# The queries' squares summed in two rounded passes, their low parts made on GpSimd

## The reference

```python
def rms_norm(x, gain):
    xf = x.astype(jnp.float32)
    xf = xf * lax.rsqrt(jnp.mean(xf * xf, axis=-1, keepdims=True) + NORM_EPS)
    return (xf * gain.astype(jnp.float32)).astype(x.dtype)
...
    q = rope(rms_norm(q.reshape(b, L, DSA_HEADS, DSA_HEAD_DIM), q_norm), positions)
    k = rope(rms_norm(k.reshape(b, L, DSA_HEADS, DSA_HEAD_DIM), k_norm), positions).reshape(b, L, bw)
```

## Time and profile before

| | us |
|---|---|
| timed runs, median of 3 | 2751.54 (2751.1 to 2751.74) |
| profiled execution, device time | 2753.97 |
| its span | 2752.2 |
| TensorE busy | 2745.2 |
| VectorE busy | 1844.5 |
| ScalarE busy | 1335.7 |
| GpSimd busy | 940.7 |

### The profile page before, as it was taken

One profiled execution on the slowest core, in us unless ns is written; L12 is line 12 of the kernel. 1 busy time (PEld: TensorE's weight loads), 2 busy tenths in 40 slices (PEclk: granted clock), 3 DMA queues, 4 the chain that ended last, 5 costly groups with the idle time before them and its releaser, 6 DMA issues.

```text
span 2752.2 us, 41841 instructions
## 1 busy us (share of the span) xinstructions
PE 2745.2 (100%) x16054; PEld 2337.4 (85%) x16054; DVE 1844.5 (67%) x2984; ACT 1335.7 (49%) x2103; POOL 940.7 (34%) x466
## 2 busy tenths in 40 slices
PE   9999999999999999999999999999999999999999
PEld 7898888777788888898988988887777888898988
DVE  6676857785657448585785878577856674585755
ACT  6353444656355446353563534446553653553533
POOL 0134824433343442131121357244333434421221
PEclk9999999999999999999999999999999999999999
DMA  5333584222222233232332335832222222323322
GB/s 171 99 104 123 148 179 115 77 77 70 85 85 84 86 94 99 92 116 99 109 108 92 116 115 155 174 108 80 74 75 79 86 85 85 100 97 95 108 98 102
DMA packets 113109, 284.80 MB, mean 103 GB/s; under 512 B 35616, under 2 KB 45344, under 8 KB 112416
## 3 DMA queue, kind: packets, MB, share of 16 engines
q1 hardware_dynamic: 112928, 282.35, 34.4%
HBM read 268.67 MB, written 9.44 MB: 101 GB/s over the span
## 4 chain that ended last, share of the span: by engine, by line
PE 97%; DVE 2%; DMA 1%; issue 0%; ACT 0%; SPq 0%; ACTq 0%; DVEq 0%
PE bank L622 22%; PE bank L624 21%; PE bank L623 21%; PE bank L671 7%; PE bank L672 7%; PE bank L673 7%; PE bank L648 1%; PE bank L650 1%; PE bank L649 1%; PE bank L1043 1%; PE bank L812 1%; PE bank L1062 1%; PE bank L1077 1%; PE bank L1176 1%; DVE da_s L2786 0%; DMA da_s<-da_qk 0%
## 5 line engine op out<-in xcount | busy, mean ns | idle before, releaser
L477 POOL TENSOR_TENSOR w_lo<-raw,w_hi 128x1024 fp32r<-128x1024 f32 x208 | 520.2, 2504 | 873.3 <-ACT w_hi L469 873.3
L622 PE MATMUL bank<-h_hi,w_hi 128*128 128x512 f32 x1504 | 593.4, 395 | 0.4 <-DVE silu_a L2358 0.3
L624 PE MATMUL bank<-h_hi,w_lo 128*128 128x512 f32 x1504 | 585.9, 390 | 0.0
L623 PE MATMUL bank<-h_lo,w_hi 128*128 128x512 f32 x1504 | 585.8, 389 | 0.0
L469 ACT ACTIVATE w_hi<-raw 128x1024 fp32r<-128x1024 f32 x310 | 326.4, 1056 | 362.5 <-PE bank L624 314.5
L542 POOL TENSOR_TENSOR w_lo<-raw,w_hi 128x1024 fp32r<-128x1024 f32 x122 | 223.5, 1853 | 805.0 <-DVE bank L2303 805.0
L622 PEld LDWEIGHTS bank<-h_hi,w_hi 128*128 128x128 f32 x1504 | 282.3, 188 | 65.2 <-issue 6.7
L624 PEld LDWEIGHTS bank<-h_hi,w_lo 128*128 128x128 f32 x1504 | 282.3, 188 | 59.7
L623 PEld LDWEIGHTS bank<-h_lo,w_hi 128*128 128x128 f32 x1504 | 282.6, 188 | 56.5
L622 PE MATMUL bank<-g_hi,w_hi 128*128 128x512 f32 x698 | 271.9, 390 | 0.0
L623 PE MATMUL bank<-g_lo,w_hi 128*128 128x512 f32 x698 | 271.7, 389 | 0.0
(11 more groups left out here) (452 smaller groups left out, 5892.5 us busy)
## 6 DMA issues: line engine op xcount, KB each, us to landing
raw<-in_w_lots SPq DMA_DIRECT2D x478, 512.0 KB, 3.7
s_wd<-s_z SPq DMA_DIRECT2D x8, 512.0 KB, 2.7
s_t<-s_taps SPq DMA_DIRECT2D x16, 256.0 KB, 13.4
da_s<-da_qk SPq DMA_DIRECT2D x16, 256.0 KB, 4.1
x<-in_x SPq DMA_DIRECT2D x8, 256.0 KB, 5.6
raw_k<-in_w_lots SPq DMA_DIRECT2D x8, 256.0 KB, 6.4
s_w_im<-s_wd SPq DMA_DIRECT2D x32, 64.0 KB, 4.0
s_w_re<-s_wd SPq DMA_DIRECT2D x32, 64.0 KB, 2.8
```

Of the source, the lines that this page charges most:

```text
L477: eng.tensor_tensor(w_lo[:, s], raw[:, s], w_hi[:, s].bitcast(f32), SUB).then_inc(S["lo_done"], 1)
L622: pe.matmul(b[:, :], w_hi[:, s, kw], xh[:, k], start=(k == 0), stop=False)
L623: pe.matmul(b[:, :], w_hi[:, s, kw], xl[:, k], start=False, stop=False)
L624: return pe.matmul(b[:, :], w_lo[:, s, kw], xh[:, k], start=False, stop=(k == nk - 1))
```

## The change

The queries' squares are split like the keys'. A step `("da_high", 0)` is put between `da_index 2` and `tokens v`: four roundings on ScalarE into four tiles that the outputs of the second half of the GLU will take later. GpSimd makes the four low parts, in place over the squares, between its split for the third and its split for the fourth value lot. TensorE makes eight fp32r passes for the queries in place of four plain matmuls. The semaphore `da_low` counts the queries' four parts ahead of the keys'.

```diff
@@ script()
-    s += [("da_index", 2), ("tokens", "v"), ("da_rope", 1, 0, 4)] + topk(1, 0, 2) + [("da_index", 3), ("da_high", 1), ("da_low", 1), ("glu", 1)]
+    s += [("da_index", 2), ("da_high", 0), ("tokens", "v"), ("da_rope", 1, 0, 4)] + topk(1, 0, 2) + [("da_index", 3), ("da_high", 1), ("da_low", 1), ("glu", 1)]
@@ tiles
-        da_lo = [None, at("da_lo_k", [P, 4, SEQ], f32r, A + 8)]
-        da_hi = [(),
+        da_lo = [at("da_lo_q", [P, 4, SEQ], f32r, 0, extra), at("da_lo_k", [P, 4, SEQ], f32r, A + 8)]
+        da_hi = [[at("da_hi_q%d" % j, [P, SEQ], f32r, Y + t) for j, t in enumerate((2, 3, 6, 7))],
                  [at("da_hi_k%d" % j, [P, SEQ], f32r, A + 4 + j) for j in range(4)]]
@@ TensorE, da_norm(g)
                 for j in range(4):
-                    if g == 0:
-                        pe.wait_ge(S["da_sq"], j + 1)
-                        pe.matmul(bank[4 + j][:, :], C("blk"), da_t[g][:, j], start=True, stop=True).then_inc(S["da_ms"], 1)
-                        continue
-                    pe.wait_ge(S["da_low"], j + 1)
+                    pe.wait_ge(S["da_low"], 4 * g + j + 1)
                     pe.matmul(bank[4 + j][:, :], blk_r[:, :], da_hi[g][j][:, :], start=True, stop=False)
                     pe.matmul(bank[4 + j][:, :], blk_r[:, :], da_lo[g][:, j], start=False, stop=True).then_inc(S["da_ms"], 1)
@@ GpSimd
+            def low_squares(g):
+                for j in range(4):
+                    pool.wait_ge(S["da_sq"], 8 + 4 * g + j + 1)
+                    pool.tensor_tensor(da_lo[g][:, j], da_t[g][:, j], da_hi[g][j][:, :].bitcast(f32), SUB) \
+                        .then_inc(S["da_low"], 1)
@@ GpSimd, mixing()
                     elif step[0] == "tokens":
                         for i in range(4):
+                            if step[1] == "v" and i == 3:
+                                low_squares(0)
                             after(step[1], i)
...
                     elif step[0] == "da_low":
-                        g = step[1]
-                        for j in range(4):
-                            pool.wait_ge(S["da_sq"], 8 + j + 1)
-                            pool.tensor_tensor(da_lo[g][:, j], da_t[g][:, j], da_hi[g][j][:, :].bitcast(f32), SUB) \
-                                .then_inc(S["da_low"], 1)
+                        low_squares(step[1])
```

## The result

| | us |
|---|---|
| before, beside it | 2751.27 median of 19 runs (2750.76 to 2752.58) |
| after | 2756.67 median of 19 runs (2755.20 to 2758.13) |
| ratio | 1.0020, 95% interval 1.0014 to 1.0026 |
| after, profiled execution | 2757.59, span 2755.8 |

The change costs 5.4 us. The forecast was +2.8, and the measured time lies 0.67 us above the upper end of the range. Of the changes predicted for TensorE's stream, all came. What was added is a piece that the prediction had as a rival: the clock.

The account below looks back on a forecast made before the run. TensorE, busy 2745.2 of 2752.2 us, was taken as the bound. Per layer -1.56 for the sums + 3.0 of bank wait gave 1.4, doubled 2.8 on the median 2751.54: 2754.3 us; range 2748.0 to 2756.0.

Parts of the forecast that it names:

- the clock: Rival: behind the 3.0 us pause before gate lot 0 TensorE's clock halves, 3.05 us lost per layer, 2757.6; chance 0.09.
- The saved 1.56 us per layer: TensorE's query sums: rounded passes of 1.87 us replace plain fp32 sums of 3.43 us, 3.1 us in all.
- ScalarE and the weights at nothing, da_low in time: ScalarE's four added roundings, 2.21 us, cost nothing; GpSimd's weight splits and low parts reach TensorE in time.
- The walk of VectorE: VectorE's queue, held by GpSimd from rope's last add on, runs 5.4 us late; third-lot glu_y ends about 516.3, not 510.4.
- The rule that two engines take turns by whole ops: A VectorE op with two SBUF inputs and a GpSimd op reading SBUF take turns for whole instructions, in issue order.
- The wait at the gate: TensorE waits 3.0 us per layer before gate lot 0, until glu_y frees its bank; start 516.3 instead of 513.34.
- a row with a pause of 0.17 us: TensorE's earlier wait at 473.27 for glu_y of the first GLU lot; called too short to tell about the clock.
- what leaves its stream is gained: Whole kernel: time taken out of TensorE's stream is gained, and time it waits is lost, one for one.
- The rival of the full gain: Rival: VectorE and GpSimd fit together better than walked, no wait before gate lot 0, 2748.4; chance 0.20.

Follow-up runs that it names:

- busy_wait: Changed kernel with twelve extra discarded TensorE passes just ahead of gate lot 0, filling the pause without shortening the bank wait; 2754.05 us, ratio 1.0011.
- after_dt_late: Changed kernel with the m2_dt product moved from the start of the attention stage to just ahead of its end; 2757.43 us, ratio 1.0021.
- glu_first: Changed kernel with VectorE making glu_y of the third GLU lot ahead of the four multiplies of da_norm(0) and y_lo; 2752.33 us, ratio 1.0004.
- passes_alone: Changed kernel without GpSimd's four query subtractions, the second pass reading the high part again; ScalarE's roundings stay; 2752.94 us, ratio 1.0006.
- the first of the two alone: Changed kernel with only VectorE's glu_y of the third GLU lot put ahead of da_norm(0), the run glu_first; 2752.33 us, ratio 1.0004.
- the second alone: Changed kernel with only the m2_dt product moved to just ahead of the attention stage's end, the run after_dt_late; 2757.43 us, ratio 1.0021.
- gpsimd_alone: Changed kernel with the query sums again plain fp32 matmuls, plus short 64-column passes; GpSimd's subtractions and ScalarE's roundings stay; 2754.56 us, ratio 1.0012.
- busy_short: Changed kernel with four extra discarded TensorE passes ahead of gate lot 0, where busy_wait has twelve; 2755.78 us, ratio 1.0014.
- glu_first_dt_late: glu_first with the m2_dt product also moved to just ahead of the attention stage's end; 2748.46 us, ratio 0.9989; run again 2748.05, ratio 0.9986.
- before_glu_first: Kernel before with only VectorE's product of the third GLU lot put ahead of the normalisation; 2751.14 us, ratio 0.9999.

## Why the prediction was wrong

- **The saved 1.56 us per layer: right.** The eight passes run from 496.14 to 497.99, 1.85 us, and TensorE is 1.6 us earlier behind them.
- **ScalarE and the weights at nothing, da_low in time: right.** No wait of TensorE for a w_lo, a w_hi or a low part was added.
- **The walk of VectorE: right at its end, 1 us too late in its middle.** On the clock of before, the scale ended at 498.0 (walked 498.3), the scores at 504.4 (505.1), y_lo at 507.2 (508.0), and the multiplies were reached at 511.1 (512.1), 4.4 us late instead of 5.4. That did not matter, because all four then stood behind the w_lo that ended at 512.6: they were done at 515.0 (515.1). The rule that two engines take turns by whole ops held in every row read here, as the Trainium skill, page "SBUF — State Buffer", section "Who interferes with whom", has it.
- **The wait at the gate: right.** 516.33 against 516.3, lost 2.99 us against 3.0. busy_wait, in which this wait is kept and the idleness isn't, measured 2754.05 against the forecast of 2754.3.
- **The step that failed is the clock's.** The prediction had it as a rival with 3.05 us per layer and 2757.6, and gave it 0.09. The profiled execution of after is this rival: 3.0 us per layer, 2757.59. Over 19 runs the median is 2756.67, because the fall doesn't follow each pause: one fall on top of busy_wait's 2754.05 would give 2755.7 and two 2757.3, and the runs lie around both (an inference from the times; all nineteen show a granted clock below 1.000). What was wrong was that the price of the clock behind a pause of 3 us was left out of the sum, as if the pause were harmless until shown otherwise, on the strength of a row with a pause of 0.17 us that said nothing either way, while the earlier trace rows showed that the clock does fall in this kernel. The Trainium skill, page "TensorE: Matmul & The Clock Gate", Part 1, says that TensorE falls to 1.2 GHz after it has been idle for a time. The pause at 513.79 was followed by that level, the equal one of after_dt_late in the second layer wasn't, so for a pause of this size the runs decide. The rival deserved more than 0.09. And as the forecast and this rival share the same pause, the range should have reached from one to the other.
- **Wrong, and without effect on the number: "what leaves its stream is gained", one for one, and with it the full gain at 2748.4.** That a late TensorE has no gap in which to make up was right: after keeps its 3.0 us to the end of the layer. An early one doesn't keep its lead. Without the pause the kernel doesn't come to 2748.4 but to 2752.3 (glu_first) or 2752.9 (passes_alone), since an earlier TensorE pulls ScalarE and GpSimd ahead into VectorE's small ops of the attention stage. In after the 3 us of pause hid that. The walk ended at the gate; another was needed where GpSimd's next three w_lo meet m2_dt. The rival of the full gain, with 0.20, was not open to this change.

## What to carry to other kernels

When TensorE becomes earlier, GpSimd's splits become earlier with it, and each of them can hold VectorE until it ends, also at an op of 0.2 us. Here the ops with two SBUF inputs and the TENSOR_SCALARs of whole blocks were held, MAX8, MATCH_REPLACE8 and the ops that read a bank were not. Walk VectorE's queue again in each later stage, not in the one that is edited alone. A new pause of TensorE of the size measured here, 1.9 to 2.9 us, is priced with its clock, 1.6 us more each time that it falls, and the range reaches from with to without. Where an edit gains nothing though its own stage shows the gain, look for the place where it is given back, and try the cures together: here the first of the two alone left 4 us lying, and the second alone gained nothing.

## What the runs showed of the hardware

- The clock fell to its lower level behind pauses of 1.9 and 2.85 us in some layers and not in others of the same execution, and not behind the two of 0.8 us in gpsimd_alone's profile. The stretch at the lower level began 0.2 us before the first matmul in the first layer of after (513.61 against 513.79), 0.8 us behind it in the second (1885.77 against 1884.98), and 1.3 us behind it in busy_short (515.20 against 513.87). A fall cost some 1.6 us.
- A VectorE op of 128x32 that takes 0.19 us alone took 2.2 us beside a GpSimd subtraction of 128x1024. Before has such a hold already: L2878 there takes 2.20 us at 530.98, and 0.19 where it is out of GpSimd's way in glu_first_dt_late. A TENSOR_SCALAR of 128x256, 0.29 us alone, took 2.05.
- The opening differs between executions: at 20 us into the span TensorE of after, of glu_first_dt_late and of before_glu_first is 2.6, 2.8 and 2.9 us ahead of the profile of before, with the code there unchanged in all of them. Profiles are compared from behind the opening on.
